# Attention kernel: mean squares as strips, loads between a row's block stores and load, value pages begun by ScalarE

## The reference, cut to what matters

```
def rms_norm(x, gain):                       # x: (..., 64) for keys and queries, one head
    xf = xf * rsqrt(mean(xf * xf) + 1e-6)
    return xf * gain
k = rms_norm(k.reshape(b, t, 16, 64), k_norm);  q = rms_norm(q.reshape(b, t, 16, 64), q_norm)
logits = where(key_pos <= q_pos, q @ k.T * scale + (c_q - c_k), -inf)
out = softmax(logits) @ v                    # then * silu(gate), output projection, residual
```

## Time and profile before

| | |
|---|---|
| median of three runs | 1516.23 us (1515.57 to 1516.42) |
| the profiled execution | 1516.44 us, its span 1514.6 us |
| TensorE busy | 1479.3 us, 98% of the span |
| VectorE, ScalarE, GpSimd busy | 991.3, 678.2, 419.9 us |
| attention | from about 735 us on; a pair is about 82 us |
| moved by DMA | 300.53 MB |

### The profile page before, as it was taken

The page is one execution under the profiler, slowest core; times in us unless marked ns, Lnnn a source line. Parts: engine busy times, 40 slices in busy tenths (PEclk is TensorE's granted clock), DMA queues, the critical chain, the costliest instruction groups (busy, mean ns, idle before and its releaser), DMA issues.

```text
span 1514.6 us, 23379 instructions
## 1 busy us (share of the span) xinstructions
PE 1479.3 (98%) x8437; PEld 1090.5 (72%) x8437; DVE 991.3 (65%) x1987; ACT 678.2 (45%) x1380; POOL 419.9 (28%) x335
## 2 busy tenths in 40 slices
PE   7999999999999999999999999999999999989998
PEld 6888888888888875446777777777777777754443
DVE  6868696877868684126377677758677676748321
ACT  4445545444445552212356555546555455545100
POOL 5012322121212101012051625443452615332200
PEclk9999999999999999999999999999999999999999
DMA  9683938466483943323247779596968778698731
GB/s 268 192 240 97 292 105 260 147 190 200 150 239 99 299 155 108 102 64 128 61 124 197 251 217 305 178 279 210 280 215 248 260 229 294 185 324 315 238 134 58
DMA packets 290505, 300.53 MB, mean 198 GB/s; under 512 B 25863, under 2 KB 247295, under 8 KB 290391
## 3 DMA queue, kind: packets, MB, share of 16 engines
q1 hardware_dynamic: 279254, 262.44, 56.8%
q0 software_dynamic: 11136, 36.59, 7.1%
HBM read 243.57 MB, written 122.53 MB: 242 GB/s over the span
## 4 chain that ended last, share of the span: by engine, by line
PE 84%; DVE 6%; ACT 5%; DMA 2%; issue 2%; SPq 1%; POOL 0%; DVEq 0%; POOLq 0%
PE psum L2134 42%; PE psum L2158 7%; PE psum L2646 7%; PE psum L2446 4%; PE psum L2472 4%; PE psum L2211 3%; PE psum L2097 2%; PE psum L2504 2%; PE psum L2406 2%; ACT psum L1274 1%; ACT psum L1283 1%; PE psum L2281 1%; PE psum L2222 1%; PE psum L2297 1%; PE psum L2299 1%
## 5 line engine op out<-in xcount | busy, mean ns | idle before, releaser
L2134 PE MATMUL psum<-arena 128*128 128x252 f32 (+1 forms) x3472 | 811.4, 384 | 2.2 <-DVE arena L1451 2.2
L2134 PEld LDWEIGHTS psum<-arena 128*128 128x128 f32 x3472 | 640.8, 190 | 124.0 <-issue 23.1
L949 POOL TENSOR_TENSOR arena<-arena 128x1024 f32<-128x1024 f32 x64 | 158.2, 2472 | 374.2 <-DMA arena<-k_pages 368.8
L1451 DVE TENSOR_TENSOR arena<-arena,psum 128x252 f32<-128x252 f32 (+1 forms) x310 | 128.8, 416 | 160.5 <-PE psum L2134 155.7
L2646 PE MATMUL psum<-arena 128*128 128x512 f32 x256 | 115.6, 604 | 4.5 <-DMA arena<-o_heads 2.9
L2158 PE MATMUL psum<-arena 128*128 128x512 f32 x256 | 113.0, 594 | 0.1
L1024 ACT COPY arena<-psum 128x252 f32<-128x252 f32 (+1 forms) x124 | 46.2, 373 | 139.5 <-PE psum L2134 139.4
L2646 PEld LDWEIGHTS psum<-arena 128*128 128x128 f32 x256 | 47.6, 192 | 63.2 <-issue 60.7
L2158 PEld LDWEIGHTS psum<-arena 128*128 128x128 f32 x256 | 47.5, 190 | 57.4 <-issue 56.5
L1087 ACT ACTIVATE arena<-arena 128x1024 f32<-128x1024 f32 x48 | 50.7, 1056 | 84.6 <-DVE arena L1497 84.2
L1274 ACT ACTIVATE psum<-psum,arena 128x640 f32<-128x640 f32 (+3 forms) x64 | 58.9, 921 | 59.9 <-DVE arena L1798 59.9
(11 more groups left out here) (272 smaller groups left out, 2086.4 us busy)
## 6 DMA issues: line engine op xcount, KB each, us to landing
k_pages<-in_cache_k SPq DMA_DIRECT2D x64, 512.0 KB, 6.5
v_pages<-in_cache_v SPq DMA_DIRECT2D x64, 512.0 KB, 7.2
arena<-k_pages SPq DMA_DIRECT2D x64, 512.0 KB, 5.3
arena<-v_pages SPq DMA_DIRECT2D x64, 512.0 KB, 6.8
arena<-in_w_in_a SPq DMA_DIRECT2D x32, 512.0 KB, 6.9
arena<-in_x_prompt SPq DMA_DIRECT2D x16, 512.0 KB, 7.5
arena<-in_w_kv SPq DMA_DIRECT2D x16, 512.0 KB, 6.6
arena<-in_w_in_b SPq DMA_DIRECT2D x16, 512.0 KB, 7.6
```

The lines of the kernel that those rows point to most:

```text
L949: pool.tensor_tensor(k_ring[:, m % 2], k_ring[:, m % 2], q_all[:, m % S:m % S + 1, :].broadcast_to([P, PAGES, P]), ALU.mult).then_inc(kq_m ...
L1451: dve.tensor_tensor(out, more, bank[n % 2][:, 0:size(u)], ALU.add).then_inc(of.by_dve, 1)
L2134: ins = pe.matmul(bank[n % 2][:, 0:size(u)], w[:, k, :], x[:, k, :], start=(k == 0 and r in (0, 1, 3, 4)), stop=(k == HK - 1), skip_group_ ...
```

## The change

- **Strips.** A set of mean squares (keys or queries of a pair) is four matmuls of 258 columns (`W4`), each with 32 columns of `bones` as weights, into four strips of 32 partitions of bank 7; in a strip the first 16 partitions have the one head's mean and the other 16 the other's. ScalarE does one Ln and one Exp over 258 columns. SP stores partitions 0, 32, 64, 96 (and 16, 48, ...) of both sets to a buffer in DRAM (`rs_out`, two DMAs), waits, and loads each head's row as a broadcast to 64 partitions (`rs_in`, two DMAs of 528 KB). Both norms wait for both loads. The semaphores of layer 0's strips are used on.
- **SP's order.** Next loads stand between a row's block stores and its load: `k_in(m + 3)` in row 4, the key and query weights in row 6. In pair 6 the first heads of the output projection are loaded (`ob_early`) that `last()` loaded before.
- **Value pages.** `v_in` is issued by ScalarE, behind `gate_ln` in row 3 and behind `soft(p, 5)` in row 5.
- **Order on VectorE and TensorE.** `scale_w` of the next key and query weights stands behind `row_max(p, 1)` and two adds; two `score` and `smp_sum` move; the norms stand behind `row_max(p, 7)`, `fin(p, 2)` and one add. On TensorE the means stand ahead of the first two `vg` units, `turn_num` behind a unit, and both first output parts of the last pair ahead of `weighted(p - 1, 3)`.

```diff
@@ -647,13 +645,28 @@
             k_in(0, 1)
-            v_in(0, 0, *range(HALF))
+            for b in range(HALF):
+                sp.dma_start(v_ring[:, b], v_pages[b, 0]).then_inc(v_loaded[b], 16)
             sp.wait_ge(c_stored, 16)
...
             hi_in(0)
+            def rs_out(q):
+                sp.wait_ge(strips_set, OUT_STRIPS + 2 * (q + 1))
+                sp.wait_ge(rs_done, 16 * OUT_STRIPS + 32 * q)
+                for x in range(2):
+                    src = sq_both[16 * x:P:32].rearrange("p (y n) -> p y n", y=2)[:, :, 0:W4]
+                    sp.dma_start(rs_rows[x].rearrange("y (s n) -> s y n", n=W4), src).then_inc(strips_stored, 16)
+            def rs_in(q):
+                sp.wait_ge(strips_stored, 16 * OUT_STRIPS + 32 * (q + 1))
+                for x, rows in enumerate(HEAD):
+                    sp.dma_start(sq_both[rows], rs_rows[x].rearrange("y n -> (y n)").partition_broadcast(DH)).then_inc(rs_done, 16)
+            rs_out(0)
+            rs_in(0)
             sp.wait_ge(b_units.done, kq_b(0, 14))
@@ -689,6 +702,13 @@
+            def ob_early(p):
+                sp.wait_ge(max_done, 2 * TT * (p + 1))
+                w_ob_in(early_b, 2)
+                sp.wait_ge(s_done, scored(p, TT - 1, 1))
+                for h in range(2):
+                    sp.dma_start(o_y[h], o_dram[h]).then_inc(early_b, 16)
             def pair(p):
@@ -698,22 +718,20 @@
                     k_in(m)
-                    v_in(p - 1, 1, *range(HALF))
                     hi_in(p)
...
                 store_row(p, 4)
+                k_in(m + 3)
                 load_row(p, 4)
-                k_in(m + 3)
                 store_row(p, 5)
                 load_row(p, 5)
-                if p:
-                    v_in(p, 0, 0, 1)
                 k_in(m + 4)
+                rs_out(p + 1)
+                rs_in(p + 1)
                 store_row(p, 6)
-                load_row(p, 6)
                 sp.wait_ge(b_units.done, kq_b(p + 1, 14))
@@ -722,22 +740,21 @@
                     sp.dma_start(o_y[2], o_dram[2]).then_inc(early_b, 16)
+                load_row(p, 6)
                 k_in(m + 5)
                 store_row(p, 7)
-                k_in(m + 6)
-                load_row(p, 7)
-                if p:
-                    v_in(p, 0, 2, 3)
+                if p + 2 == PAIRS:
+                    ob_early(p)
+                    load_row(p, 7)
+                    k_in(m + 6)
+                else:
+                    k_in(m + 6)
+                    load_row(p, 7)
...
                 k_in(m - 1)
-                sp.wait_ge(max_done, 2 * TT * p)
-                w_ob_in(early_b, 2)
-                sp.wait_ge(s_done, scored(p - 1, TT - 1, 1))
-                for h in range(2):
-                    sp.dma_start(o_y[h], o_dram[h]).then_inc(early_b, 16)
                 k_in(m)
@@ -1204,16 +1218,19 @@
-            def rs_ln(q, y, *ns):
-                for n in ns:
-                    act.wait_ge(items.done, items.at(f"m{'kq'[y]}{n}", q))
-                    act.activation(sq[y][:, part3(n)], bank[7][:, 0:W3], ACT.Ln, bias=eps).then_inc(items.taken, 1)
-            def rs_out(q, y):
-                act.wait_ge(items.taken, items.at(f"m{'kq'[y]}2", q))
-                act.activation(sq[y], sq[y], ACT.Exp, scale=-0.5).then_inc(rs_done, 1)
+            def v_in(p, g):
+                act.wait_ge(num_done, 2 * p + g)
+                for b in range(HALF):
+                    act.dma_start(v_ring[:, b], v_pages[HALF * g + b, p]).then_inc(v_loaded[b], 16)
+            def rs_strips(q, y):
+                n = items.at("m" + "kq"[y], q)
+                act.wait_ge(items.done, n)
+                act.activation(sq[y][:, 0:W4], bank[7][:, 0:W4], ACT.Ln, bias=eps).then_inc(items.taken, 1)
+                act.wait_ge(items.taken, n)
+                act.activation(sq[y][:, 0:W4], sq[y][:, 0:W4], ACT.Exp, scale=-0.5).then_inc(strips_set, 1)
@@ -1346,6 +1360,8 @@
                 gate_ln(p)
+                if p:
+                    v_in(p - 1, 1)
                 soft(p, 4)
@@ -1354,27 +1370,21 @@
                 soft(p, 5)
+                if p:
+                    v_in(p, 0)
                 if nxt:
...
                     squares(p + 1, 1)
-                if nxt:
-                    rs_ln(p + 1, 0, 0)
+                    rs_strips(p + 1, 0)
                 vg(0)
                 if nxt:
-                    rs_ln(p + 1, 0, 1)
+                    rs_strips(p + 1, 1)
                 soft(p, 6)
                 vg(2)
-                if nxt:
-                    rs_ln(p + 1, 0, 2)
-                    rs_ln(p + 1, 1, 0)
-                    rs_out(p + 1, 0)
-                    rs_ln(p + 1, 1, 1)
-                if nxt:
-                    rs_ln(p + 1, 1, 2)
-                    rs_out(p + 1, 1)
                 soft(p, 7)
...
                 dec_e(p, 0)
+            v_in(PAIRS - 1, 1)
             dec_e(PAIRS - 1, 1)
@@ -1926,10 +1936,10 @@
             vg_add(0, 3)
-            norm(0, 0)
             vg_add(0, 4)
...
             vg_add(0, 6)
+            norm(0, 0)
             dve.wait_ge(raw_set, 1)
@@ -1955,23 +1965,26 @@
                     score(m - 4)
-                    score(m - 3)
                 vg_add(p, 10)
                 turn_v(p, 0)
+                row_max(p, 1)
+                vg_add(p, 11)
+                vg_add(p, 12)
                 if nxt:
...
                     scale_w(dve, w_q, gain_b, p + 1, w_q_loaded, w_q_scaled)
-                row_max(p, 1)
-                vg_add(p, 11)
-                vg_add(p, 12)
+                if p:
+                    score(m - 3)
                 vg_add(p, 13)
...
                     score(m - 2)
+                kq(1)
+                if p:
+                    score(m - 1)
                     smp_sum(p - 1, 0)
-                kq(1)
                 turn_v(p, 2)
@@ -1980,7 +1993,6 @@
                 if p:
-                    score(m - 1)
                     tops(p - 1, 1)
@@ -2025,14 +2037,13 @@
                 vg(4)
+                row_max(p, 7)
+                fin(p, 2)
                 if nxt:
                     norm(p + 1, 0)
-                row_max(p, 7)
+                vg(5)
                 if nxt:
                     norm(p + 1, 1)
-                fin(p, 2)
-                vg(5)
-                if nxt:
                     top_of(p, 0)
@@ -2399,11 +2410,13 @@
-            def means(q, y, *ns):
-                for n in ns:
-                    dst = open_item(f"m{'kq'[y]}{n}", q)
-                    pe.wait_ge(sq_done, 2 * q + y + 1)
-                    pe.matmul(dst[:, 0:W3], bones, sq[y][:, part3(n)], start=True, stop=True, skip_group_check=True).then_inc(items.done, 1)
+            def means(q, y):
+                dst = open_item("m" + "kq"[y], q)
+                pe.wait_ge(sq_done, 2 * q + y + 1)
+                for n in range(4):
+                    ins = pe.matmul(dst[32 * n:32 * n + 32, 0:W4], bones[:, DH - 16:DH + 16], sq[y][:, n * W4:(n + 1) * W4],
+                                    start=True, stop=True, skip_group_check=True)
+                ins.then_inc(items.done, 1)
@@ -2539,24 +2552,23 @@
                 kq_n(0)
+                last((0, 0, 3), (1, 0, 3))
                 if p:
...
                 kq_n(1)
-                last((0, 0, 3))
                 turn_values(p, 0)
...
                 turn_rows(p, 2)
-                if p:
-                    turn_num(p - 1, 0)
                 turn_values(p, 1)
                 kq_n(2)
+                if p:
+                    turn_num(p - 1, 0)
                 turn_vs(p)
...
                 kq_n(4)
-                last((1, 0, 3))
                 weighted(p, 0)
@@ -2587,27 +2599,20 @@
-                def means_n(y, n):
-                    if nxt:
-                        means(p + 1, y, n)
                 scores(p, 6)
-                means_n(0, 0)
+                if nxt:
+                    means(p + 1, 0)
                 vg_n(0)
-                means_n(0, 1)
+                if nxt:
+                    means(p + 1, 1)
                 vg_n(1)
...
                 last((2, 7, 8), (3, 0, 8))
-                means_n(0, 2)
-                vg_n(3)
-                means_n(1, 0)
-                vg_n(4)
-                means_n(1, 1)
+                vg_n(3, 4)
...
                 weighted(p, 2)
-                means_n(1, 2)
                 vg_n(5)
```

60 lines of the change are left out of this document (23 added, 37 removed).

## The result

The changed kernel takes 1532.22 us (median of four runs, 1531.41 to 1532.98) beside 1516.33 of the kernel before (the median of four runs; the 1516.23 further up is that of three): a ratio of 1.0105, 95% interval 1.0091 to 1.0119. It is slower by 15.9 us; the forecast was 1497.0, its range ended at 1511.

A forecast was written before the change was run, and what follows sets the result against it. TensorE, busy for 98% of the span, was taken as the bound. Means -21.7, waits 7 x (0.3 + 0.4), first pair +1.0 and last pair -3.3 sum to -19.1: 1516.44 gives 1497.3, median 1497.1 us; range 1487 to 1511.

The forecast's parts named there:

- The mean squares: On TensorE, four side-by-side strips replace three matmuls a set: 0.57 us a set, 21.7 us gained in all.
- The round trip: Roots go to DRAM and back before VectorE's norms: landed at 1066.6, 3 us of cover, 0.3 us of wait a pair.
- rival A: VectorE's norm waits for the roots' broadcast, landing 1.8 late, x 7 = 13 us, so 1510; chance 0.13.
- Value pages ... at nothing: ScalarE issues four value loads in its idle time before row 4 and before the squares; priced at nothing.
- Between the store and load of a row ... nothing on the path: SP issues next loads while it waits anyway for a row's store to land; no cost.
- VectorE's order (0.4 a pair): In rows 0 to 3 the later weight scaling cuts the cover of GpSimd's sums from 4.7 us to 0.2; 0.4 a pair.
- rival C: GpSimd's sums come late for TensorE's second unit, 1.5 us a pair, so 1505; chance 0.13.
- Start and first pair: First pair's means gain 2.4 us; its norms, with factors at about 746.5, make TensorE wait 1.0 once.
- The last pair (-3.3): Waits for blocks and heads and slow records go, 6.3 us; a new wait in row 3 costs 3.0; net 3.3.
- Rival B: Same place as the norm's wait, but 3.3 us late a pair, slower than before: 1520; chance 0.06.

The follow-up runs named there:

- the short broadcast: Changed kernel with the two broadcasts of the roots loading 64 of 2064 elements a partition, so most norm factors are wrong; 1521.89 us, ratio 1.0034.
- the fastest version: Changed kernel with row 3's value loads on SP, row 4's key page behind that row's load, roots' stores ahead of row 5's load; 1504.76 us, ratio 0.9926.

## Why the prediction was wrong, step by step
Two steps failed that the prediction had priced at nothing: the value loads on ScalarE (9.3 us) and SP's new order between a row's store and load. A third, the round trip, was priced too short (4.3 us a pair over, against a cover of 3). The gain of the strips themselves came.
- **The mean squares: right.** A set takes 0.58 us on the timeline (1066.93 to the next unit at 1067.51) against 0.57 forecast; 10.3 us busy is inside 9 to 11. The Trainium skill's 3.07 for four row tiles ("TensorE: Matmul & The Clock Gate", "Part 3: Packing small matmuls") would make the busy time of a set an estimated 4 x 0.47 / 3.07 = 0.61; the row says 10.3 / 16 = 0.64, which is nearer to the page's figure than to my 0.47. From start to start, which is what the sum goes by, the 0.57 held. TensorE's busy time fell by 12.3, not 20 to 25: it holds other changes too, among them stretches at the lower clock, and the rest was not taken apart. With the short broadcast rows 6 and 7 give 2.3 a pair, against 2.45 (2.75 - 0.3) forecast.
- **The round trip: rival A came true, at 0.13, as a mechanism.** (Its own terms add up to a landing at 1071.1, not 1071.4.) The stores went out when forecast, but for one pair of seven (7.7 behind row 6's start). From them to the broadcasts I had 3.0 us (1057.5 to 1060.5), a light store's low end of 2.3 with its issue; it was 4.7 to 5.4 in six of seven pairs. I had looked at how heavy the stores were, not at what SP had put ahead of them: `load_row(p, 5)`, which waits for landed stores, and a key page, 1.3 MB in all. With the stores issued first it is 2.4. The broadcasts then took 8.0 to 8.2 until the norm, where it waited, and I had 6.1. Together 4.3 over, against a cover of 3: waits of 1.2 to 3.3 a pair (A priced 1.8). The price by the short broadcast is 10.3 us, the start in it, by A 13. Until SP's order was put right this row could only get longer: 15.5 in the run with the key page behind row 4's load.
- **"Value pages ... at nothing": wrong.** The issues took 1.78 and 1.82 us as forecast and hid. What I priced was ScalarE's time, and not the 2 MB in front of SP's next key page, which before went out 13.4 us behind the values (1017.80 and 1031.15) and now 2.5, and was used 6.1 to 7.6 us after its issue instead of 3.8 to 4.7 with the loads back on SP. Cost: 9.3 us. The Trainium skill's rule that I had quoted for rival A ("DMA: Bandwidth & Descriptors", "Issuing engines are not separate DMA queues") was borne out, in row 3 and not where I applied it.
- **"Between the store and load of a row ... nothing on the path": wrong.** It moved GpSimd's product onto the gate: 1.3 us a pair in the run with the value loads back. I had no term for VectorE slowing down beside GpSimd. And in the queue as changed, the load of row 5 stands ahead of the roots' stores: once row 5 was short, they went out 7.8 to 8.5 behind row 6's start instead of 5.8, in six of seven pairs.
- **VectorE's order (0.4 a pair), rival C:** no second unit waited in the middle pairs; once, in the first (3.2), and the old order takes 3.4 us off that pair. Right for the middle pairs, a miss for the first. The new order does let a 64-column product start beside GpSimd's (6.1 us of L2494), which is row 3's 1.3: gone with the old order alone, and with the value loads back alone.
- **Start and first pair:** forecast -2.4 + 1.0, measured +2.0 and +2.6. I had the factors there at 746.5; the broadcasts went out at 741.67 and VectorE waited for them until 750.80, so the first scores waited 2.9. With the short broadcast they start at 751.0, and not at 753.4. Row 0 pays 1.7 for the lower clock behind that wait, and row 2 pays 3.4, rival C's wait.
- **The last pair (-3.3): wrong, +0.2.** Both waits are gone (0.2 of 4.9 left) and the granted clock of 1354 to 1358 is 1.00, not 0.61; its row 2 takes 5.2 less. But row 3 took 1.7 back: the wait forecast at 3.0 came, at 3.4 (L2485). And row 5 took 3.1. There VectorE waits 3.3 for GpSimd's product, which starts at 1393.23 because its key page came late, ahead of the row's maximum, and the granted clock of 1392 to 1396 is 0.58. With row 3's value loads on SP this row is 2.4 shorter.
- **Rival B** had the right sign and the wrong shape: the trip alone was not 2.8 late in the mean (1.6 over the seven pairs, 3.3 at most). Slower came from three causes in three rows, none of them big enough alone.
- **Scale:** a pair is 84.0 us, not 82; I took one window for the mean.

What stays open: in the fastest version the first pair is still 2.5 us longer than before, and VectorE waits 13.4 us for roots. The old VectorE order would take 3.4 off the first pair, but no run had it in that pair alone. That a transfer came late by the bytes ahead of it is read from the times of issue and use and from what moving them did, not from the transfers themselves.

## What to carry to other kernels
A step that only takes "an issue" must be read in the queue that issues it: what that queue waits for just ahead of it, and how many bytes it has put in front. A small store that starts a chain goes ahead of a bulk load that has to wait; here that one swap was worth 22.6 us, from 1527.32 to 1504.76. And when a saving does not show, look for the row in which it comes back: the chain that ends there is the next thing to move.

## What the runs showed of the hardware
- VectorE instructions of two SBUF operands stand still beside a product or a sum of GpSimd: 64 columns 226 ns before, 1099 in the mean after (2.56 us in the pair shown), 8 columns 159 and 1510, and 222 for the 64 when GpSimd's products were small. In the held cases VectorE's end follows that of GpSimd's instruction.
- Loads in ScalarE's queue delay SP's: a 512 KB key page issued 2.5 us behind 2 MB was used 7.6 us after its issue (3.8 to 4.7 in the middle pairs with these loads back on SP), and 2 MB beside two broadcasts stretched these from 6.4 to 9.6 us.
- From the issue of two small stores to the loads that wait for their landing: 5.0 us behind 1.3 MB of loads, 2.4 ahead of them; the broadcasts that follow were used after 7.9 and 10.2.
- Behind TensorE's waits of 2.88 and 2.18 us the granted clock was 0.57 and 0.51, its lower level of 1.2 GHz for most of the stretch; eight records of 264 columns took 3.36 us behind the first and 2.05 at full clock. Behind a wait of 2.67 at the same place, in the run with row 5's values behind row 7, it stayed at 1.00.
- Eight records of four strips of 258 columns span 0.64 us, where one matmul of 252 takes 0.46.
